# A fused two-block transformer kernel: order of values, scores and weight splits in the first block's head loop

## The chip, the cores and the metric

The kernel runs on one core of a Trainium2 chip. The time is that of the device for one execution, in microseconds (us). The engines are TensorE (PE, with its weight loads shown as PEld), VectorE (DVE), ScalarE (ACT), GpSimd (POOL) and SyncE (SP), which here only issues transfers.

## The reference

`x` has 512 tokens of 2048 features. The first block is sliding-window attention with 32 heads of 64 in 4 key/value groups, attention sinks, ALiBi and an output gate. The second block (two layers) is latent attention, a short convolution and memory attention, with a gate; it isn't touched here. Cut to the first block:

```
h = rmsnorm(x, g_pre)
q, k, v, z = split(h @ w_in)                     # 2048, 256, 256, 2048 columns
scores = q.k / 8 - slope * dist, masked to a window of 128, in blocks of 128 queries by 256 keys
p = softmax(concat(scores, sink))[..., :-1]
o = p @ v
y = (o * silu(z)) @ w_out
x = x + rmsnorm(y, g_post)
```

## The kernel before

Every weight matrix is handled in chunks of 2048 x 128 (1 MB), alternating between two slots of `raw`, `hi`, `lo` and `acc`. For each chunk SP loads `raw`; ACT writes `hi`, a rounded copy (`split` on ACT, L1147); DVE writes `lo = raw - hi` (`split` on DVE, L1599); PE then multiplies (`features`, L631): 16 k-tiles, each of three matmuls of 128 x 512 (hi by h_hi, hi by h_lo, lo by h_hi) into `acc[slot]`. A chunk can be split only when the chunk two before is multiplied (`chunk_done`), and multiplied only when `lo_done` says that it is split and `evacuated` that its accumulator has been read.

The first block's loop runs over 16 head pairs. Pair i has a q chunk (slot 0) and a gate chunk z (slot 1). Pair 0 stands before the loop, pairs 1 to 13 in it, and pairs 14 (`A`) and 15 (`B`) are written out behind it, where the order of chunks is q_a, q_b, z_a, z_b. In pair i:

- DVE scales q from the accumulator (`q_scaled`, L1786), ACT writes its high half (L1222), DVE its low half (`q_low`, L1792), which raises `q_split`.
- Inside the z chunk, ahead of k-tile 6, PE runs `scores_first(i)`: 16 matmuls of 256 columns (L781, L782). They wait for `q_split` and for POOL's copies of k (L533, L537).
- DVE runs `softmax_front(i)`: for each of the pair's two heads a large scalar_tensor_tensor over 128 x 1024 (L1747, scores from PSUM, `win` from SBUF), a maximum (L1749) and three tiny instructions (L1750 to L1752); ACT takes the exponentials (L1229, L1231); `softmax_back(i)` sums, inverts, scales (L1761 to L1764) and transposes 32 x 32 blocks into `pt1` (L1768).
- SP moves the transposed probabilities out to DRAM in two transfers (L390) and back in four (L393), `move_first(i)`. In SP's queue they stand between the load of a q chunk and the load of a gate chunk.
- Inside the z chunk of pair i+1, ahead of k-tile 10, PE runs `values_first(i)`: 16 matmuls (L795) with 64-column weights. They wait for the four transfers (`pt1_in`), for POOL's copy of v (`vcur`, L544) and for the earlier y product.
- DVE forms the y product (`y_first`, L1776, two instructions) and the gate (`gate_first`: L1802 reads the z accumulator and releases it, ACT takes tanh, L1237, DVE closes with L1806).

Each engine executes its own instructions in the order in which they are written. DVE's order for pair i before: split of z_i, q, split of q_(i+1), softmax_front(i), y_first(i-1), softmax_back(i), gate_first(i). Behind the loop it is: split of q_b, q(14), split of z_a, softmax_front(14), y_first(13), softmax_back(14) with the scaling of q_b inside, q_low(15), split of z_b, softmax_front(15), softmax_back(15). PE runs scores(14) and values(13) in q_b, scores(15) ahead of k-tile 10 of z_a, values(14) ahead of k-tile 3 of z_b.

Of the kernel before, what the change touches and what calls it, by code (L numbers as in the profile page):

```python
# [22 lines left out]
def build(nc, xT, memT, mem, pos, gains, gain_row, sinks, consts, window, w1, w2, out):  # L23
# [7 lines left out]
    ACT = mybir.ActivationFunctionType  # L31
# [4 lines left out]
    D, S, MEM = 2048, 512, 256  # L36
# [8 lines left out]
    PAIR1 = 4  # L45
# [40 lines left out]
    def chunk1(p, i=0):  # L86

        new = isinstance(i, int) and i == 0 and p < 2
        return Chunk(i * 2 + p, p % 2, i + p // 2, i + p // 2, None if new else 2)
# [57 lines left out]
    with ctx:  # L147
# [473 lines left out]
        def _(pe):  # L621
# [31 lines left out]
            def features(c, x_hi, x_lo, meanwhile=(), last_reader=False):  # L653

                begin(c)
                for k in range(KT):
                    for pause, other in meanwhile:
                        if k == pause:
                            other()
                    ins = k_tile(c, k, x_hi, x_lo, k == 0, k == KT - 1)  # L660
                    if last_reader and k == KT // 2 - 1:
                        ins.then_inc(h_half_read, 1)
                ins.then_inc(chunk_done, 1)
# [110 lines left out]
            def scores_first(i):  # L774
                pe.wait_ge(q_split, i + 1)
                pe.wait_ge(kcur_done, i * 3 + 3)
                for b in range(TB):
                    for par in range(2):
                        to = bank(2 * par + b // 2, 256, b % 2 * 256)
                        q, k = tile(par * TB + b, P), slice(b * P, b * P + 256)  # L780
                        pe.matmul(to, q1[:, q], k_hi[:, k], start=True, stop=False)  # L781
                        ins = pe.matmul(to, q1[:, q], k_lo[:, k], start=False, stop=True)  # L782
                ins.then_inc(scores1, 1)

            def values_first(i):
                pe.wait_ge(pt1_in, i * (QUADS * 16) + QUADS * 16)
                pe.wait_ge(vcur_done, i * 2 + 2)
                pe.wait_ge(y1, i + 1)
                for kb in range(TB):
                    at, n = 2 * kb * BLK, (2 if kb < TB - 1 else 1) * BLK  # L790
                    for par, rows_ in enumerate(HALVES):
                        to = ov[par][rows_, kb * P:kb * P + QUADS * n].rearrange("p (b a i) -> p a b i", a=QUADS, i=BLK)
                        src = pt1[:, 0:T1].rearrange("p (a n x) -> p a n x", a=QUADS, n=2)[:, :, par, at:at + n]
                        src = src.rearrange("p a (b i) -> p a b i", i=BLK)
                        ins = pe.matmul(to, vcur[:, kb * P + par * HD:kb * P + (par + 1) * HD], src,  # L795
                                        start=kb == 0, stop=kb == TB - 1, skip_group_check=True)
                ins.then_inc(values1, 1)

            def pair(i, first):

                features(chunk1(PAIR1, i), h_hi, h_lo,
                         meanwhile=[(9, lambda: spread(1, ov[1][:, 0:MEM], MEM, zt))] if first else [])
                features(chunk1(PAIR1 + 1, i), h_hi, h_lo,
                         meanwhile=[(6, lambda: scores_first(i))] if first else
                         [(6, lambda: scores_first(i)), (10, lambda: values_first(i - 1))])

            pair(0, True)
            with pe.Fori(1, A) as i:
                pair(i, False)
            features(q_a, h_hi, h_lo)  # L810
            features(q_b, h_hi, h_lo, meanwhile=[(6, lambda: scores_first(A)), (10, lambda: values_first(A - 1))])
            features(z_a, h_hi, h_lo, meanwhile=[(10, lambda: scores_first(B))])
            features(z_b, h_hi, h_lo, meanwhile=[(3, lambda: values_first(A))], last_reader=True)

# [327 lines left out]
        def _(act):  # L1142
            def split(c, width=CW):
                act.wait_ge(loaded[c.slot], (c.uses + 1) * 16)
                if c.back is not None:
                    act.wait_ge(chunk_done, c.n + (1 - c.back))
                act.activation(hi[c.slot][:, 0:width], raw[c.slot][:, 0:width], ACT.Copy).then_inc(hi_done, 1)  # L1147
# [70 lines left out]
            def q_hi(i, qc):  # L1218
                act.wait_ge(evacuated[qc.slot], qc.accs + 1)
                act.wait_ge(scores1, i + 1)  # L1220
                for par, half_ in enumerate(HALVES):
                    ins = act.activation(q1[half_, tile(par)], qt[half_, :], ACT.Copy)  # L1222
                ins.then_inc(q_hi_done, 1)

            def exps_first(i):
                for par in range(2):
                    act.wait_ge(shift1, i * 2 + (par + 1))
                    for n in range(par * TB, par * TB + TB):
                        act.activation(prob1[:, tile(n, 256)], prob1[:, tile(n, 256)], ACT.Exp,  # L1229
                                       bias=nm[:, n:n + 1], accum_out=ls[:, n:n + 1])  # L1230
                    act.activation(es[:, tile(par, TB)], es[:, tile(par, TB)], ACT.Exp).then_inc(exp1, 1)  # L1231

            def tanh_first(i, zc, first=False):
                act.wait_ge(evacuated[zc.slot], zc.accs + 1)
                if not first:
                    act.wait_ge(sg_done, i)
                act.activation(tz, zt[:, :], ACT.Tanh, scale=0.5).then_inc(tanh1, 1)  # L1237

            def pair(i, first):
                qc, zc = chunk1(PAIR1, i), chunk1(PAIR1 + 1, i)  # L1240
                split(zc)
                q_hi(i, qc)
                split(chunk1(PAIR1 + 2, i))
                exps_first(i)
                tanh_first(i, zc, first)

            pair(0, True)
            act.wait_ge(r_done, 2)
            act.activation(ones_r[:, :], ones, ACT.Copy)
            act.activation(r_mem[:, :], ov[1][:, 0:MEM], ACT.Copy).then_inc(r_mem_done, 1)  # L1250
            with act.Fori(1, A) as i:
                pair(i, False)
            split(q_b)
            q_hi(A, q_a)
            split(z_a)
            exps_first(A)
# [339 lines left out]
        def _(dve):  # L1596
            def split(c, width=CW):
                dve.wait_ge(hi_done, c.n + 1)
                dve.tensor_tensor(lo[c.slot][:, 0:width], raw[c.slot][:, 0:width], hi[c.slot][:, 0:width].bitcast(F32),  # L1599
                                  ALU.subtract).then_inc(lo_done, 1)  # L1600
# [140 lines left out]
            def softmax_front(i):  # L1741
                dve.wait_ge(scores1, i + 2)
                for par in range(2):
                    link = Links(soft1_link, i * 12 + par * 3)
                    half_, part = tile(par, 1024), tile(par, TB)
                    sink = snk[:, col(i * 2 + par)]
                    link.then(dve.scalar_tensor_tensor(prob1[:, half_], win[:, :], cst[:, col(i * 2 + (SLOPE + par))], sc[:, half_],  # L1747
                                                       ALU.mult, ALU.add))
                    link.then(dve.tensor_reduce(mx[:, part], prob1[:, half_].rearrange("p (n k) -> p n k", n=TB), AX.X, ALU.max))  # L1749
                    link.then(dve.tensor_scalar(mx[:, part], mx[:, part], sink, None, ALU.max))  # L1750
                    dve.tensor_scalar(es[:, part], mx[:, part], -1.0, sink, ALU.mult, ALU.add)
                    dve.tensor_scalar(nm[:, part], mx[:, part], -1.0, None, ALU.mult).then_inc(shift1, 1)  # L1752
# [47 lines left out]
            def gate_first(i, zc, meanwhile=None):  # L1800
                dve.wait_ge(chunk_done, zc.n + 1)
                dve.tensor_tensor(zt[:, :], acc[zc.slot][:, :], r_x[:, :], ALU.mult).then_inc(evacuated[zc.slot], 1)  # L1802
                if meanwhile is not None:
                    meanwhile()
                dve.wait_ge(tanh1, i + 1)
                dve.scalar_tensor_tensor(sg, tz, 1.0, zt[:, :], ALU.add, ALU.mult).then_inc(sg_done, 1)  # L1806

            def pair(i, first):
                zc = chunk1(PAIR1 + 1, i)
                split(zc)  # L1810
                q(i, chunk1(PAIR1, i))
                split(chunk1(PAIR1 + 2, i))
                softmax_front(i)
                if not first:
                    y_first(i - 1)
                softmax_back(i)
                gate_first(i, zc)

            def y_lo_tile(t, count):
                dve.wait_ge(y_hi_done, count)  # L1820
# [1 line left out]
                                  ALU.subtract).then_inc(y_done, 1)  # L1822

            dve.wait_ge(window_in, 32)
            pair(0, True)
            dve.wait_ge(x_stored, 16)
            with dve.Fori(1, A) as i:
                pair(i, False)
            split(q_b)
            q(A, q_a)  # L1830
            split(z_a)
            softmax_front(A)
# [688 lines left out]
```

## Time and profile before

| | us |
|---|---|
| median of 3 runs | 2197.26 (2196.68 to 2197.3) |
| the profiled execution | 2197.51 |
| its span | 2195.7 |
| PE busy | 2178.5 |
| PEld busy | 1818.9 |
| DVE busy | 1524.7 |
| ACT busy | 837.5 |
| POOL busy | 211.3 |

The span is the time from the first to the last instruction of the trace; the execution's own time is 1.8 us longer. Busy times are sums over the engine's instructions; matmul ends are modelled, so a short stop of PE can lie hidden between two matmuls whose records overlap, and the starts of the matmuls show it better. The granted clock of TensorE is at full speed, 0.999 on the mean. The head loop runs from about 60 to 480 us of the span.

### The profile page before, as it was taken

Reading aid. Unit: us, or ns where it says so; the run is one execution under the profiler, and the core shown is the slowest. Engines: PE = TensorE matmul, PEld = TensorE weight load, DVE = VectorE, ACT = ScalarE, POOL = GpSimd, SP = SyncE. Lnnn points to the kernel's source line nnn. Section 1 sums busy time; section 2 is a strip of 40 time slices with the busy share of each in tenths; the row PEclk is TensorE's granted clock in tenths of the full one; section 3 lists DMA queues with packets and bytes.
Section 4 is the critical chain, followed back from the end, with each engine's and each line's share of the span. In section 5 each row is a group of like instructions: output and inputs, shape, how many; then the busy total and the mean of one; then the engine's idle time right before and its main releaser. Section 6 shows DMA issues by size and latency. Waiting matters only on the chain.

```text
span 2195.7 us, 27821 instructions
## 1 busy us (share of the span) xinstructions
PE 2178.5 (99%) x10428; PEld 1818.9 (83%) x10428; DVE 1524.7 (69%) x2224; ACT 837.5 (38%) x1307; POOL 211.3 (10%) x215
## 2 busy tenths in 40 slices
PE   8999999999999999999999999999999999999998
PEld 7888888888888888888888888888888888888887
DVE  6677788888988543567677778786434677677665
ACT  6433433453345421334333533444213443435221
POOL 0100000114420100000000053201000000000000
PEclk9999999999999999999999999999999999999999
DMA  7445545442257223225443422573222154435532
GB/s 278 172 154 155 159 157 160 146 149 96 89 213 273 78 96 100 75 75 160 134 139 119 142 107 82 194 268 113 96 96 75 65 158 132 144 117 155 176 119 108
DMA packets 91019, 303.25 MB, mean 138 GB/s; under 512 B 7536, under 2 KB 48752, under 8 KB 67888
## 3 DMA queue, kind: packets, MB, share of 16 engines
q1 hardware_dynamic: 84912, 275.00, 38.0%
q10 hardware_dynamic: 4896, 17.30, 2.1%
q0 software_dynamic: 1120, 9.70, 1.2%
q8 instruction: 61, 1.00, 0.2%
q14 instruction: 30, 0.25, 0.0%
HBM read 253.74 MB, written 48.23 MB: 138 GB/s over the span
## 4 chain that ended last, share of the span: by engine, by line
PE 98%; DMA 1%; DVE 1%; issue 0%; ACT 0%; SPq 0%; DVEq 0%; POOLq 0%; POOL 0%; ACTq 0%
PE acc L631 69%; PE sc L631 11%; PE ov L631 6%; PE sc L855 3%; PE sc L856 2%; PE ov L795 1%; PE sc L782 1%; PE sc L781 1%; PE sc L1038 1%; PE sc L1037 1%; DMA g<-xT_dram 0%; PE acc L816 0%; PE acc L817 0%; PE acc L647 0%; PE acc L820 0%
## 5 line engine op out<-in xcount | busy, mean ns | idle before, releaser
L631 PE MATMUL acc<-h_all,hi 128*128 128x512 f32 x4160 | 1286.9, 391 | 8.9 <-DVE h_all L1691 8.9
L631 PEld LDWEIGHTS acc<-h_all,hi 128*128 128x128 f32 x4160 | 775.6, 188 | 170.5 <-issue 12.0
L631 PE MATMUL acc<-h_all,lo 128*128 128x512 f32 x2080 | 809.9, 389 | 0.0
L1599 DVE TENSOR_TENSOR lo<-raw,hi 128x2048 fp32r<-128x2048 f32 (+3 forms) x158 | 345.1, 2184 | 171.3 <-ACT hi L1147 169.2
L631 PEld LDWEIGHTS acc<-h_all,lo 128*128 128x128 f32 x2080 | 390.8, 188 | 81.9
L1147 ACT ACTIVATE hi<-raw 128x2048 fp32r<-128x2048 f32 (+3 forms) x158 | 289.1, 1830 | 430.5 <-PE acc L631 263.8
L1229 ACT ACTIVATE prob<-prob,st 128x256 f32<-128x256 f32 x128 | 63.6, 498 | 109.4 <-DVE st L1752 109.4
L631 PE MATMUL sc<-hi,h_all 128*128 128x512 f32 (+1 forms) x320 | 90.7, 369 | 0.0
L1306 ACT ACTIVATE hi<-raw 128x512 fp32r<-128x512 f32 x50 | 30.4, 627 | 120.7 <-PE sc L856 107.5
L631 PEld LDWEIGHTS sc<-hi,h_all 128*128 128x128 f32 x320 | 58.1, 189 | 10.4 <-issue 0.5
L1542 ACT ACTIVATE prob<-sc,st 128x512 f32<-128x512 f32 x64 | 44.2, 690 | 43.6 <-DVE st L2299 43.6
L496 POOL TENSOR_TENSOR sqacc<-sqacc,sq 128x512 f32<-128x512 f32 x28 | 53.4, 1907 | 57.9 <-ACT sq L1161 56.4
L631 PE MATMUL sc<-lo,h_all 128*128 128x512 f32 (+1 forms) x160 | 58.8, 368 | 0.0
L1154 ACT ACTIVATE hi<-raw 128x1024 fp32r<-128x1024 f32 x32 | 32.2, 1054 | 68.4 <-PE acc L631 54.3
L855 PE MATMUL sc<-t_parts,hi 128*128 128x512 f32 x160 | 57.8, 398 | 0.0
L2238 DVE TENSOR_TENSOR pt_low<-pt,pt_hi 128x1024 fp32r<-128x1024 f32 x32 | 37.8, 1222 | 25.8 <-ACT pt_hi L1504 25.8
L555 POOL TENSOR_TENSOR t_raw<-g 128x512 f32<-128x512 f32 x4 | 7.1, 1778 | 484.8 <-DVE lo L1599 484.8
L1504 ACT ACTIVATE pt_hi<-pt 128x1024 fp32r<-128x1024 f32 x32 | 32.1, 1052 | 48.4 <-DMA pt<-turned 48.4
L2298 DVE TENSOR_REDUCE st<-sc 128x1 f32<-128x512 f32 x64 | 44.1, 689 | 7.6 <-PE sc L1038 5.1
L1161 ACT ACTIVATE sq<-g 128x512 f32<-128x512 f32 x64 | 38.7, 627 | 22.5 <-POOL qacc L500 7.6
L608 POOL DMA_DIRECT2D cs<-gain_row_dram x1 | 0.6, 623 | 481.6 <-ACT h_all L1164 481.6
L2362 DVE STREAM_TRANSPOSE x_rows<-x_piece 32x512 f32<-32x512 f32 x64 | 45.0, 703 | 2.6 <-DMA x_piece<-residual 0.8
(331 smaller groups left out, 3399.3 us busy)
## 6 DMA issues: line engine op xcount, KB each, us to landing
raw<-w_dram SPq DMA_DIRECT2D x170, 1024.0 KB, 4.9
turned<-pt SPq DMA_DIRECT2D x32, 512.0 KB, 3.2
pt<-turned SPq DMA_DIRECT2D x64, 256.0 KB, 5.1
turned<-pt SPq DMA_DIRECT2D x32, 448.0 KB, 3.0
pt<-turned SPq DMA_DIRECT2D x64, 224.0 KB, 4.0
xr<-residual ACTq DMA_DIRECT2D x16, 512.0 KB, 5.2
residual<-g ACTq DMA_DIRECT2D x16, 512.0 KB, 4.7
raw<-w_dram SPq DMA_DIRECT2D x8, 896.0 KB, 6.6
```

Of the source, the lines that this page charges most:

```text
L496: pool.tensor_tensor(to[:, :], to[:, :], sq[:, tile(slot)], ALU.add).then_inc(added, 1)
L631: ins = pe.matmul(to, a, b, start=first and n == 0, stop=last and n == 2)
L855: pe.matmul(bank(bank_).rearrange("p (s n) -> p s n", s=2), high_, both, start=first and m == 0, stop=end, skip_group_check=True)
L856: ins = pe.matmul(bank(bank_, TILES), low_, both[:, 0, :], start=False, stop=end, skip_group_check=True)
L1147: act.activation(hi[c.slot][:, 0:width], raw[c.slot][:, 0:width], ACT.Copy).then_inc(hi_done, 1)
L1161: act.activation(sq[:, tile(slot)], src, ACT.Square).then_inc(squared, 1)
L1229: act.activation(prob1[:, tile(n, 256)], prob1[:, tile(n, 256)], ACT.Exp, bias=nm[:, n:n + 1], accum_out=ls[:, n:n + 1])
L1542: act.activation(prob2[:, tile(b)], bank(b), ACT.Exp, scale=MLA_SCALE, bias=nm[:, b:b + 1], accum_out=ls[:, b:b + 1]).then_inc(exp2, 1)
L1599: dve.tensor_tensor(lo[c.slot][:, 0:width], raw[c.slot][:, 0:width], hi[c.slot][:, 0:width].bitcast(F32), ALU.subtract).then_inc(lo_done, 1)
L2238: dve.tensor_tensor(keys_half(pt2_low, n), keys_half(pt2, n), keys_half(pt_hi, n).bitcast(F32), ALU.subtract)\
L2298: link.then(dve.tensor_reduce(mx[:, one], bank(b), AX.X, ALU.max))
L2362: dve.transpose(to[:, 4 * c:4 * c + 4, :, a, :], from_[:, :, :, q, :]).then_inc(x_turned, 1)
```

## The change

In the loop's z chunks and in q_b, the values of the pair before now stand ahead of k-tile 6 and the scores ahead of k-tile 7. On DVE softmax_back(i) follows softmax_front(i) directly; then comes the split of the next pair's gate weights (which moves from the next pair's start), then y_first(i-1), then gate_first(i). ACT's split of these weights moves likewise, from the next pair's start to directly behind the exponentials and ahead of tanh. The first gate chunk is split before pair 0, and the split of q_b that stood behind the loop is now the last one in it. Two small ACT copies (`ones_r`, `r_mem`) move from behind pair 0 into it. SP's and POOL's code is the same.

```diff
                 features(chunk1(PAIR1 + 1, i), h_hi, h_lo,
                          meanwhile=[(6, lambda: scores_first(i))] if first else
-                         [(6, lambda: scores_first(i)), (10, lambda: values_first(i - 1))])
+                         [(6, lambda: values_first(i - 1)), (7, lambda: scores_first(i))])
...
-            features(q_b, h_hi, h_lo, meanwhile=[(6, lambda: scores_first(A)), (10, lambda: values_first(A - 1))])
+            features(q_b, h_hi, h_lo, meanwhile=[(6, lambda: values_first(A - 1)), (7, lambda: scores_first(A))])
...
             def pair(i, first):                       # ACT
                 qc, zc = chunk1(PAIR1, i), chunk1(PAIR1 + 1, i)
-                split(zc)
                 q_hi(i, qc)
+                if first:
+                    act.wait_ge(r_done, 2)
+                    act.activation(ones_r[:, :], ones, ACT.Copy)
+                    act.activation(r_mem[:, :], ov[1][:, 0:MEM], ACT.Copy).then_inc(r_mem_done, 1)
                 split(chunk1(PAIR1 + 2, i))
                 exps_first(i)
+                split(chunk1(PAIR1 + 3, i))
                 tanh_first(i, zc, first)
 
+            split(chunk1(PAIR1 + 1))
             pair(0, True)
-            act.wait_ge(r_done, 2)
-            act.activation(ones_r[:, :], ones, ACT.Copy)
-            act.activation(r_mem[:, :], ov[1][:, 0:MEM], ACT.Copy).then_inc(r_mem_done, 1)
             with act.Fori(1, A) as i:
                 pair(i, False)
-            split(q_b)
...
             def pair(i, first):                       # DVE
-                zc = chunk1(PAIR1 + 1, i)
-                split(zc)
                 q(i, chunk1(PAIR1, i))
                 split(chunk1(PAIR1 + 2, i))
                 softmax_front(i)
+                softmax_back(i)
+                split(chunk1(PAIR1 + 3, i))
                 if not first:
                     y_first(i - 1)
-                softmax_back(i)
-                gate_first(i, zc)
+                gate_first(i, chunk1(PAIR1 + 1, i))
...
+            split(chunk1(PAIR1 + 1))
             pair(0, True)
             dve.wait_ge(x_stored, 16)
             with dve.Fori(1, A) as i:
                 pair(i, False)
-            split(q_b)
```

## Rows read from the trace of the kernel before

**Rows 1.** The page, busy time of each engine.
```profile
PE 2178.5 (99%) x10428; PEld 1818.9 (83%) x10428; DVE 1524.7 (69%) x2224; ACT 837.5 (38%) x1307; POOL 211.3 (10%) x215
```

**Rows 2.** Waits of PE's weight loads, 80 to 500 us: total us, times, longest.
```profile
PEld ov L795 <- issue: 5.6, 16, 0.4
PEld acc L631 <- issue: 2.7, 16, 0.2
PEld acc L631 <- DVE lo L1599: 0.2, 1, 0.2
```

**Rows 3.** Timeline of PE, one loop period: start us, duration us, instruction, count.
```profile
220.20 0.62 PE L631 MATMUL acc<-h_all,hi 128*128 128x512 f32 x2
...
224.28 0.28 PE L781 MATMUL sc<-k_hi,q 128*128 128x256 f32 x1
...
226.08 0.28 PE L782 MATMUL sc<-k_lo,q 128*128 128x256 f32 x1
...
228.72 0.39 PE L631 MATMUL acc<-h_all,lo 128*128 128x512 f32 x1
229.03 1.73 PE L795 MATMUL ov<-pt,vcur 128*64 128x256 f32 x16
...
231.50 0.62 PE L631 MATMUL acc<-h_all,hi 128*128 128x512 f32 x2
...
249.87 0.28 PE L781 MATMUL sc<-k_hi,q 128*128 128x256 f32 x1
```

**Rows 4.** Timeline of DVE over the same period, idle before in brackets.
```profile
226.66 1.27 DVE L1747 SCALAR_TENSOR_TENSOR prob<-win,cst,sc 128x1024 f32<-128x1024 f32 x1
...
232.77 0.47 DVE L1751 TENSOR_SCALAR st<-st,snk 128x4 f32<-128x4 f32 x1
...
233.22 1.38 DVE L1776 SCALAR_TENSOR_TENSOR g<-ov,sq 64x512 f32 x2
...
238.80 1.11 DVE L1768 STREAM_TRANSPOSE pt<-prob 128x896 f32<-128x896 f32 x1
239.94 0.69 DVE L1802 TENSOR_TENSOR zt<-acc,sqacc 128x512 f32<-128x512 f32 x1
241.33 0.69 DVE L1806 SCALAR_TENSOR_TENSOR sq<-sq,zt 128x512 f32<-128x512 f32 x1 [0.70 <-ACT sq L1237]
243.14 2.29 DVE L1599 TENSOR_TENSOR lo<-raw,hi 128x2048 fp32r<-128x2048 f32 x1 [1.11 <-ACT hi L1147]
...
248.10 1.39 DVE L1792 TENSOR_TENSOR q<-dg,q 64x512 fp32r<-64x512 f32 x2 [1.42 <-ACT q L1222]
```

**Rows 5.** ACT and POOL over this period; line L1751: ns min/median/max.
```profile
235.32 0.19 ACT L1231 ACTIVATE st<-st 128x4 f32<-128x4 f32 x1
...
232.58 0.63 POOL L537 CAST k_lo<-k_lo_all 64x512 fp32r x1 [0.26 <-POOL k_hi L533]
...
L1751 DVE TENSOR_SCALAR st<-st,snk x26: 228/347/624, 101.6 to 411.9; 128x4 f32<-128x4 f32 x26
```

**Rows 6.** SP's queue in this period; time from issue to landing of L393.
```profile
242.90 1.76 SPq L393 DMA_DIRECT2D pt<-turned  x4
245.61 0.36 SPq L357 DMA_DIRECT2D raw<-w_dram  x1
...
DMA to landing us min/median/max: 3.1/4.1/5.0
```

**Rows 7.** Behind the loop: DVE, PE's weight load, the fourth transfer, its landing.
```profile
431.30 1.27 DVE L1747 SCALAR_TENSOR_TENSOR prob<-win,cst,sc 128x1024 f32<-128x1024 f32 x1
...
444.84 1.39 DVE L1792 TENSOR_TENSOR q<-dg,q 64x512 fp32r<-64x512 f32 x2
...
448.54 1.28 DVE L1747 SCALAR_TENSOR_TENSOR prob<-win,cst,sc 128x1024 f32<-128x1024 f32 x1
...
446.28 0.19 PEld L781 LDWEIGHTS sc<-k_hi,q 128*128 128x128 f32 x1
...
424.33 0.43 SPq L393 DMA_DIRECT2D pt<-turned  x1
...
pt<-turned SPq DMA_DIRECT2D x1, 224.0 KB, 4.3
```

## The prediction, made before the changed kernel was run

> **What bounds the kernel now.** I read the page's busy line first: TensorE (PE) is busy for all but 17 us of the span [rows 1]. Then the waits of the PE weight loads between 80 and 500 us, the stretch that the change touches: one wait for a DVE weight split, 0.2 us, and short stops around each values group [rows 2]. So the loop is at PE's own rate and has nearly nothing to give back; what matters is whether the new order makes PE wait. For that I read one period on PE [rows 3], then DVE, ACT, POOL and SP over the same period [rows 4 to 6], then the loop's exit [rows 7]. The period is 249.87 - 224.28 = 25.59 us. The gate chunk starts at 220.20 (call this z0) and scores are six tiles later, 4.08 us, so a k-tile is 0.68 us. A values group starts 0.08 us late (228.72 to 229.03 is 0.31 where 0.23 is the pitch), and it and the tile behind it take 231.50 - 229.03 = 2.47 us. DVE has slack, but in two places little: its split of the next gate weights ends at 243.14 + 2.29 = 245.43, and PE loads weights for that chunk at about 220.20 + 25.59 - 0.23 = 245.56; the low half of q ends at 248.10 + 1.39 = 249.49, and PE loads for the scores at 249.87 - 0.23 = 249.64.
>
> **PE's own work.** The loop issues the same matmuls. Values stood between two accumulation tiles and still do: at tiles 6 and 7 one k-tile lies between values and scores. So the same switches are paid: 0 us. As bounds, dropping the 0.08 us and the weight load's stop behind each group (2.7 us / 16 = 0.17) [rows 2] would give 14 x 0.25 = 3.5 us; paying them once more would cost as much. The rows have the same neighbours, so I take 0.
>
> **Where scores and softmax land in the loop.** New scores start at z0 + 4.08 + 0.08 + 2.47 = z0 + 6.63, instead of z0 + 4.08. The group's first to last start is 226.08 - 224.28 = 1.80 and the last matmul lasts 0.28, so they end at z0 + 8.71 and DVE's first softmax instruction starts near z0 + 8.75 = 228.95. Before, it started at 226.66 [rows 4]: 2.29 us later. From there to the y product took 233.22 - 226.66 = 6.56. In it one tiny tensor_scalar (L1751) took 0.47, beside a POOL copy, where the shortest of its line takes 0.23 [rows 4, 5]. In the new order POOL copies vcur directly after values and k after scores, beside the first large softmax instruction, so I take 6.32 (bounds 6.32 and 6.56). The Trainium skill's GPSIMD Engine Reference, Specifications, says that POOL's SBUF interface is shared with VectorE and contends when DVE has two SBUF inputs or a two-port mode. The large instruction reads win from SBUF and scores from PSUM, so by that rule it is spared too; if it were slowed like L1751, the margin below would be gone. The y products (two, 1.39 together) now stand behind; softmax back takes 239.94 - 233.22 - 1.41 = 5.31. ACT's exponentials ended at 235.32 + 0.19 [rows 5] and now end 2.05 to 2.29 us later, by 237.8; DVE needs the second half's at half of 5.31 behind 235.27, 237.9. They hide, if by little; 0.3 us would be lost at worst. The second transpose, before 238.80 + 1.11 = 239.91, now ends at 228.95 + 6.32 + 5.31 - 0.03 = 240.55: 0.64 us later.
>
> **The added risk: probabilities for values.** Values were due at z0 + 8.83; they are now due at z0 + 25.59 + 4.16 = 249.95, 4.67 us earlier in the chunk. SP's queue is q weights, two transfers out, four in, gate weights. The second out goes at the transpose's end (239.91), the first in follows at 242.90, 2.99 later [rows 6]; the fourth is issued some 1.3 later (1.76 for all four) and lands up to 5.0 after its issue: about 249.2. Plus 0.64 that is 249.85, against 249.95. The margin is 0.1 us (0.25 with the loop's usual 4.9 and the first decimal of the view). I take a loop stall of 0. The gate weight load now waits for nothing (its split is done before) and goes directly behind the four transfers, 0.9 us nearer to them than 245.61 is to 242.90 + 1.76. I know no row with this order that landed later, and cost it at 0, at worst 0.3 us per period. The skill's DMA: Bandwidth & Descriptors, Anatomy of one DMA, fits a transfer as 2.0 us plus bytes over 436 GB/s. By it a 448 KB out is 3.05 us, as the trace has (2.99), but four loads of 224 KB would have landed 4.1 us after the first issue, where the trace has 6.3; by the page values would have 2 us to spare, and the loop rival below would have no chance. The measurement decides.
>
> **Splits, y, gate.** ACT's split of the next gate weights follows the exponentials: 237.6 + 1.9 = 239.5, before DVE is free at 240.55. DVE: split to 242.9, y to 244.3, gate product to 245.0. PE needs that accumulator and those weights at 245.56, so 0.55 us are left for the accumulator (its product ended at 240.6 before) and 2.7 us for the weights (0.13 before). Tanh and the second gate product end near 244.3 + 241.33 - 239.94 + 0.69 = 246.4, where q's chunk is done near 246.0; so q's scaling starts up to 0.4 later and q's low half ends at 249.9; the scores need it only at 245.79 + 6.4 = 252.2. All hidden. The 0.2 us wait of [rows 2] goes; it is one of a weight load, which hides most of it behind the matmuls in flight, so I take 0 (at most -0.2). The two small ACT copies of pair 0 move ahead of q_1's weight split; no values group follows in that pair, so its softmax may be late by their time: 0.
>
> **The exit of the loop.** This is where I find a cost. The values of the loop's last head pair, values(13) during q_b, are due at 424.92 (scores at 249.87 + 7 x 25.59 = 429.00, less 4.08) + 4.16 = 429.08. Their fourth transfer was issued at 424.33 and landed 4.3 later, 428.63 [rows 7]; this iteration issues it late. Plus 0.64 and 0.05 for the signal: 429.32, a stall of 0.24. Scores(14) then end at 429.32 + 2.47 + 2.08 = 433.87 and DVE's softmax starts at 433.91 instead of 431.30: 2.61 later. From 431.30 to the low half of q_b at 444.84 + 1.39 = 446.23 DVE runs without a gap (softmax front, y, softmax back with q_b's scaling in it, low half), and this order is not changed. PE's scores(15) at z_a's tile 10 wait for it already: their weight load is at 446.28, 0.05 behind DVE, and only 0.06 later than it would be without a wait. With DVE 2.61 later, PE waits to 448.89: PE loses 2.6 us, the 0.24 included. Then all else moves with it: DVE's z_b split and next softmax (448.54 before) by the same 2.6, and the values of head pair 14, whose transfers follow softmax back directly, keep the place that they have to them now. PE is the bound to the end of the span [rows 1], so nothing gives it back.
>
> **Sum.** +2.6 (exit, one time) + 0 (PE's work) + 0 (loop, splits) = +2.6 us. The profiled execution took 2197.51 us for a span of 2195.7, so 2200.1 for one like it; it lies 0.25 above the median, 2197.26. Predicted: 2199.9 us. A difference under 0.2%, 4.4 us, is about what a measurement of this kernel can't tell from none.
>
> **Rivals.**
> A. The loop is caught by the probabilities. From scores' end the ring is DVE, transfers out and in, values, one tile, scores; I make it 25.59 - 0.1. Each 0.1 us over that costs 12 x 0.1, from head pair 1 on. With L1751's 0.24 back: +0.14 a period, 1.7 us, 2201.6. With 0.3 us of transfer contention alone: +0.2, 2.4 us, 2202.3. With both: 0.44 x 12 = 5.3, 2205.2. It is slower by over 0.2% from 0.15 us a period on (1.8 us). For it: the margin is smaller than the spread of landings (4.7 to 5.0 over the iterations). Against: these landings are steady, and the first three transfers already keep all DMA engines busy, so that a load behind them has little to push aside. Chance 0.27, of which 0.19 over the 0.2%.
> B. No loss at the exit: scores(15) doesn't wait, or DVE makes up the 2.6 us. The time is 2197.2. For it: PE's gap there is only 0.06 us in the trace and a releaser is not named. Against: DVE has no idle time on that stretch to make up with. Chance 0.08.
> C. Values and scores near each other save the switches: 14 x 0.25 = 3.5 us against the 2.6: 2196.4; with B as well 2193.8, below the 0.2%. For it: PE pays 0.25 us a group. Against: a k-tile lies between. Chance 0.07.
> The forecast itself has 0.58.
>
> The range goes from 2196.8 (B, half of C) to 2203.0 (A with either cause alone, by nothing more); 2 in 10 or less stay outside. Slower by over 0.2% 0.19, faster 0.03, within 0.78.
>
> **What would show it.** In the changed profile: PE's wait for DVE's q low half before the last scores group, 2.4 us, and a small one for transfers before values(13); loop period 25.59 still; gate split ending 2.7 us ahead of PE; the gate product ending half a us ahead of it. The prediction is wrong if the period is longer (A), if PE waits at the gate chunk's start for the accumulator, or if scores(15) start without a wait.

## The result and the profile after

The changed kernel takes 2204.62 us (median of 7, 2202.59 to 2206.24) against 2197.3 before: a ratio of 1.0032, 95% interval 1.0022 to 1.0041. That is slower, clear of the noise, and above the stated range (2196.8 to 2203.0). Its executions also scatter more: 3.6 us from first to last, before 1.5. The profiled execution took 2202.66 us, near the lowest, for a span of 2200.8. So what follows in this section accounts for 5.15 of the 7.3 us; part of the rest shows in the trace of the run with the gate weight load held back.

PE's work is the same as in [rows 1], the rest of the longer span is time in which it stands still:

```profile
PE 2179.9 (99%) x10428; PEld 1821.5 (83%) x10428; DVE 1518.6 (69%) x2224; ACT 837.2 (38%) x1307; POOL 215.3 (10%) x215
```

The waits of PE and of its weight loads between 80 and 500 us (total us, times, longest), to set beside [rows 2]. Before, there was no wait of PE's matmuls in this stretch:

```profile
PE sc L781 <- DVE q L1793: 2.1, 1, 2.1
PE ov L795 <- DMA pt<-turned: 0.6, 2, 0.4
PE ov L795 <- issue: 0.5, 3, 0.2
...
PEld ov L795 <- issue: 7.2, 14, 0.8
...
PEld sc L781 <- DVE q L1793: 2.5, 1, 2.5
PEld ov L795 <- DMA pt<-turned: 0.7, 2, 0.4
```

Two costs can be read: one stop of 2.1 us before a scores group, and many small ones before values groups. The small ones are mostly not shown as waits, since the record of the matmul before still overlaps; the starts show them. PE's timeline, one loop period, as in [rows 3], with the first and last scores group of the loop:

```profile
100.00 0.28 PE L781 MATMUL sc<-k_hi,q 128*128 128x256 f32 x1
...
251.62 0.39 PE L631 MATMUL acc<-h_all,lo 128*128 128x512 f32 x1
252.14 1.73 PE L795 MATMUL ov<-pt,vcur 128*64 128x256 f32 x16
...
254.60 0.28 PE L781 MATMUL sc<-k_hi,q 128*128 128x256 f32 x1
...
277.75 1.73 PE L795 MATMUL ov<-pt,vcur 128*64 128x256 f32 x16
...
280.22 0.28 PE L781 MATMUL sc<-k_hi,q 128*128 128x256 f32 x1
...
434.73 0.28 PE L781 MATMUL sc<-k_hi,q 128*128 128x256 f32 x1
```

Before the values group at 252.14 the gap is 0.52 us where it was 0.31. Scores to scores over the loop is (434.73 - 100.00) / 13 = 25.75 us, before 25.59. The stops beyond the usual 0.09 sum to 2.6 us over the 14 values groups from 97.54 on, of which 0.5 stands before the first.

DVE in this period, as in [rows 4]:

```profile
256.83 1.28 DVE L1748 SCALAR_TENSOR_TENSOR prob<-win,cst,sc 128x1024 f32<-128x1024 f32 x1 [2.35 <-PE sc L782]
...
262.94 0.23 DVE L1752 TENSOR_SCALAR st<-st,snk 128x4 f32<-128x4 f32 x1
...
267.31 1.11 DVE L1769 STREAM_TRANSPOSE pt<-prob 128x896 f32<-128x896 f32 x1
268.35 2.25 DVE L1600 TENSOR_TENSOR lo<-raw,hi 128x2048 fp32r<-128x2048 f32 x1
270.52 1.38 DVE L1777 SCALAR_TENSOR_TENSOR g<-ov,sq 64x512 f32 x2
271.93 0.69 DVE L1803 TENSOR_TENSOR zt<-acc,sqacc 128x512 f32<-128x512 f32 x1
```

and SP's queue, as in [rows 6]:

```profile
271.42 1.76 SPq L393 DMA_DIRECT2D pt<-turned  x4
273.38 0.36 SPq L357 DMA_DIRECT2D raw<-w_dram  x1
```

DVE waits for scores, runs the softmax in one piece, and the second transpose ends 11.59 us after its start (forecast 11.60). The small instruction took 0.23 here instead of 0.47. The transfers in are issued 3.00 us behind it, and the gate weight load 0.2 us behind the last of them.

This is a ring: scores 254.60, softmax 256.83 (2.23), transposes 268.42 (11.59), transfers in 271.42 (3.00), values 277.75 (6.33), scores 280.22 (2.47), together 25.62 us. PE's own period is 25.59. The ring is the longer one, by 0.03 here and by 0.16 on the mean. The 6.33 us from the first transfer in to the values are 6.10 until the last of the four has landed, at 277.52, and 0.23 until PE's first matmul.

The stop behind the loop, with DVE's start of softmax(14), its low half of q_b, and PE's weight load for scores(15), as in [rows 7]:

```profile
436.84 1.28 DVE L1748 SCALAR_TENSOR_TENSOR prob<-win,cst,sc 128x1024 f32<-128x1024 f32 x1 [2.12 <-PE sc L782]
...
450.39 0.69 DVE L1793 TENSOR_TENSOR q<-dg,q 64x512 fp32r<-64x512 f32 x1
...
451.83 0.19 PEld L781 LDWEIGHTS sc<-k_hi,q 128*128 128x128 f32 x1 [2.51 <-DVE q L1793]
```

DVE starts when scores(14) end and then runs nearly without a gap; PE waits for what it does last.

### The profile page after: what moved, and what is told of

The parts are those of the page before. It is cut to its first block, busy times and chain, and to the rows that moved or that the text cites. A ratio compares the mean times of both kernels' runs of the same rounds, so it can differ in the third digit from the quotient of the medians.

```text
span 2200.8 us, 27834 instructions
## 1 busy us (share of the span) xinstructions
PE 2179.9 (99%) x10428; PEld 1821.5 (83%) x10428; DVE 1518.6 (69%) x2224; ACT 837.2 (38%) x1307; POOL 215.3 (10%) x215
## 4 chain that ended last, share of the span: by engine, by line
PE 95%; DVE 3%; DMA 1%; issue 1%; SPq 0%; ACT 0%; POOL 0%; DVEq 0%; POOLq 0%
PE acc L631 65%; PE sc L631 12%; PE ov L631 6%; PE sc L855 3%; PE sc L856 2%; PE ov L795 1%; PE sc L781 1%; PE sc L782 1%; PE sc L1038 1%; PE sc L1037 1%; DMA pt<-turned 0%; DMA g<-xT_dram 0%; PE acc L816 0%; PE acc L817 0%; PE acc L650 0%
## 5 line engine op out<-in xcount | busy, mean ns | idle before, releaser
L1748 DVE SCALAR_TENSOR_TENSOR prob<-win,cst,sc 128x1024 f32<-128x1024 f32 x32 | 40.9, 1277 | 32.9 <-PE sc L782 32.9
L544 POOL COPY vcur<-vall 128x256 f32 x32 | 17.2, 562 | 312.8 <-PE ov L795 312.5
```

## The experiments

All are timed beside the kernel before on the same chip; its median was 2197.4, 2197.46 and 2197.35 us in the three groups.

**The changed kernel again**, beside the next three.

> The changed kernel once more, on the chip of the three others, to have its time beside theirs and a second trace. Ring theory (loop bound by the ring scores, softmax, transfers, values, one tile, scores): 2202.6 to 2206, more spread than before, with the period near 25.75 us and up to 25.95 in slower executions, and one stop of 2.1 to 2.5 us before scores(15). If the 2 us between the profiled execution and the median are noise of the first runs, it comes at 2202.7.

2205.61 us (5 runs, 2202.83 to 2207.48), ratio 1.0035 (1.0022 to 1.0049). Its profiled execution took 2203.56: the period is (435.48 - 100.79) / 13 = 25.75 again, the stop before scores(15) 2.1 us again. The result repeats; most executions again lie above the profiled one. Of the changed kernel's 12 executions in both groups four have a mean granted clock of 0.998 or less, and they took 2205.61 to 2207.48 us; the other eight took 2202.59 to 2205.61, their median is 2204.0. What the lower mean stands for is seen in the trace of the run with the gate weight load held back.

**Exit: q_b's old placement.**

```diff
-            features(q_b, ..., meanwhile=[(6, lambda: values_first(A - 1)), (7, lambda: scores_first(A))])
+            features(q_b, ..., meanwhile=[(6, lambda: scores_first(A)), (10, lambda: values_first(A - 1))])
```

> Only q_b's placement goes back: scores(14) ahead of tile 6, values(13) ahead of tile 10. Exit theory (scores(15) wait for DVE, which started softmax(14) 2.2 to 2.6 us late): 2.1 to 2.4 us less than the changed kernel, no stop before scores(15), loop as in the changed kernel (2202.3 by its median). If DVE is late there for another reason (the loop's own lateness of q), less than 1 us is gained.

2201.69 us (11 runs, 2200.21 to 2203.52), ratio 1.0019 (1.001 to 1.0028), 3.9 below the changed kernel beside it, 2.9 below its first median. PE's waits, 80 to 500 us:

```profile
PE ov L795 <- DMA pt<-turned: 1.9, 4, 0.9
PE sc L781 <- DVE q L1793: 0.2, 1, 0.2
```

The stop before scores(15) goes from 2.1 to 0.2 us (by the starts from 2.24 to 0.41); the loop's stay, with a mean period of 25.76. The exit is a cause of its own. The medians gave more than the 2.1 to 2.4 expected. All 11 executions have a mean granted clock of 0.999; against the eight of the changed kernel with 0.999 or more the gain is 2.3 us, the size that was expected.

**Values and scores next to each other.**

```diff
-                         [(6, lambda: values_first(i - 1)), (7, lambda: scores_first(i))])
+                         [(6, lambda: values_first(i - 1)), (6, lambda: scores_first(i))])
(and in q_b likewise)
```

> Values and scores both ahead of tile 6, values first, in the loop and in q_b: the one k-tile between them goes, everything else as in the changed kernel. Ring theory: the ring is 0.68 us shorter, so 25.1 to 25.3 against PE's 25.59: the loop's stalls vanish (-2.1 against the trace, up to -4.8 against the median), and the exit's is 0.7 less; 2198.8 to 2199.5. Contention theory (the gate weight load behind the four transfers delays them by a varying amount): the stall is mostly gone too, but landing times are above 5.0 in some periods. Switch theory (PE loses by the new neighbours, not by waits): no gain over the changed kernel, 2203 to 2205.

2200.3 us (11 runs, 2198.87 to 2202.55), ratio 1.001 (1.0001 to 1.0019). Twelve periods in a row are 25.55 or 25.56 us:

```profile
252.40 0.39 PE L631 MATMUL acc<-h_all,lo 128*128 128x512 f32 x1
252.72 1.73 PE L795 MATMUL ov<-pt,vcur 128*64 128x256 f32 x16
254.38 0.39 PE L781 MATMUL sc<-k_hi,q 128*128 128x256 f32 x1
...
278.27 1.74 PE L795 MATMUL ov<-pt,vcur 128*64 128x256 f32 x16
```

Scores now start 1.66 us behind values, before 2.47. This takes 0.8 us out of the ring and ends every stall inside the loop: values come 0.32 us after the tile before, as in the kernel before. What stays is at the ends: 0.7 us before values(0), 0.6 before values(13), 1.4 before scores(15) (1.6 by the starts). The median came 0.8 us above the upper end of what I expected; I had priced none of the first two. The profiled execution is the slowest of its 11, 2202.55 us: its granted clock was half from 14.3 to 17.7 us of the span, long before the loop, and its scores(0) start at 74.92, 2.3 us later than in the kernel before. By their starts the new neighbours also save PE 0.03 us a period.

**DVE's and ACT's order alone.**

```diff
-                         [(6, lambda: values_first(i - 1)), (7, lambda: scores_first(i))])
+                         [(10, lambda: values_first(i - 1)), (6, lambda: scores_first(i))])
(and in q_b likewise)
```

> DVE's and ACT's new order alone; on PE scores ahead of tile 6 and values ahead of tile 10 as before. Ring theory: values are due 2.7 + 3.4 us later in the ring than they were in the changed kernel, so no stall, and the exit has none: 2197.3, within 0.3 us of before. If DVE's new order costs by itself (gate product late for PE, q late for the scores: both still have over half a microsecond in the changed trace, but scores are due 2.55 us earlier here, at z0 + 4.08, where q's low half ends at about z0 + 4.1): 0.1 to 0.3 us a period, up to 2201.

2197.4 us (11 runs, 2197.01 to 2198.37), ratio 1.0 (0.9991 to 1.0009), no wait of PE's matmuls in the stretch, periods of 25.59. This half of the change costs nothing and gives nothing: PE is the bound without it. The loss comes with PE's placement; how large it gets depends on DVE's order, as the next two runs show.

**PE's placement alone**, on the kernel before.

```diff
-                         [(6, lambda: scores_first(i)), (10, lambda: values_first(i - 1))])
+                         [(6, lambda: values_first(i - 1)), (7, lambda: scores_first(i))])
(and in q_b likewise)
```

> PE's new placement (values at 6, scores at 7) with DVE's and ACT's order of before. Ring theory: y_first (1.41) and the slowed small instruction (0.24) stand in the ring again, and, longer still, the gate weight split comes last on DVE: from softmax start 13.28 to the gate product, 3.2 to the split, 2.3 for it, and then PE's 6 tiles, values, tile, scores: about 27.8 us a period by my sum, 2.2 over PE's 25.59. 13 periods make 28 us: 2224 to 2228 with the exit. Contention or switch theory: DVE's order matters only in slack, so within 2 us of the changed kernel, 2203 to 2207.

2226.87 us (4 runs, 2226.18 to 2226.95), ratio 1.0135 (1.0119 to 1.0151). The waits name the ring that I had taken for the longer one, through the split of the gate weights, and the period is (430.64 - 99.29) / 12 = 27.61 us, against my 27.8:

```profile
PE acc L631 <- DVE lo L1599: 22.6, 13, 1.7
PE sc L781 <- DVE q L1792: 2.1, 1, 2.1
```

With PE's new placement DVE's and ACT's new order is worth 21 to 22 us (2226.87 against 2204.62 and 2205.61); with the old placement it is worth nothing.

**y between the two halves of softmax**, in the changed kernel.

```diff
                 softmax_front(i)
+                if not first:
+                    y_first(i - 1)
                 softmax_back(i)
                 split(chunk1(PAIR1 + 3, i))
-                if not first:
-                    y_first(i - 1)
```

> The changed kernel with y_first back between softmax front and back; the gate weight split stays ahead. Ring theory: the transposes come 1.41 to 1.65 us later and the ring, which binds already, grows by all of it: 12 or 13 x 1.4 to 1.65 = 17 to 21 us over the changed kernel, 2222 to 2226; PE waits for the transfers, not for DVE's split. If the loop isn't a ring and only the due time of the values counts, one such delay is paid once a period too, but not more than 0.2 to 0.4 us behind the slack: 2205 to 2209.

2222.7 us (4 runs, 2222.02 to 2224.79), ratio 1.0115 (1.0099 to 1.0131), 17 to 18 over the changed kernel:

```profile
PE ov L795 <- DMA pt<-turned: 22.9, 15, 2.7
PE sc L781 <- DVE q L1793: 2.1, 1, 2.1
```

Work of 1.4 us put into the ring comes out in every period, whose mean over 12 goes from 25.76 to 27.25: the ring binds already. With the split ahead, PE waits for the transfers and no longer for the split, so the two rings of the last experiment are told apart.

**Both three tiles earlier**, one tile between them as in the changed kernel.

```diff
-                         [(6, lambda: values_first(i - 1)), (7, lambda: scores_first(i))])
+                         [(3, lambda: values_first(i - 1)), (4, lambda: scores_first(i))])
(and in q_b likewise)
```

> The changed kernel with values ahead of tile 3 and scores ahead of tile 4, in the loop and in q_b. Both move three tiles (2.04 us) forward in the chunk together. Ring theory: the ring's length is the same, so the loop's stalls are as before this edit; at the exit DVE starts softmax(14) only 0.5 us later than in the kernel before instead of 2.6, so the stop before scores(15) shrinks by 2.0: 2202.5 to 2203.7. Due-time theory (values are due 2.04 us earlier in the chunk, transfers come when they come): 12 x 2 us more, 2225 or over.

2202.26 us (10 runs, 2201.8 to 2204.39), ratio 1.0023 (1.0014 to 1.0033). Values are due 2 us earlier in every chunk, and the loop's period is (408.00 - 98.58) / 12 = 25.79 us, against 25.75 before the edit. The place in the chunk costs nothing, the distance from values to scores does. Once, the earlier place is paid: 1.6 us before values(0), since pair 0 has its scores ahead of tile 6 still. The stop before scores(15) is nearly gone, 0.2 us by the starts.

```profile
PE ov L795 <- DMA pt<-turned: 3.5, 5, 1.6
PE ov L795 <- issue: 0.3, 2, 0.2
...
PEld sc L781 <- DVE q L1793: 0.5, 1, 0.5
```

**The gate weight load behind the landed transfers.**

```diff
                 move_first(i - 4)
+                sp.wait_ge(pt1_in, i * (QUADS * 16) - 3 * (QUADS * 16))
                 load1(1, i)
```

> The changed kernel, but SP issues the gate weight load only when the four transfers of probabilities have landed (one more wait in SP's queue), so nothing runs behind them. Contention theory: landings become shorter and steadier; 1.5 to 4 us less than the changed kernel (2201 to 2203) and less spread. Ring theory with uncontended transfers (the landings in the changed trace, 4.8 to 5.0, are those of before): no change, 2204 to 2206, and the same spread. The load itself has some 13 us to spare until its split.

2202.14 us (11 runs, 2200.31 to 2203.31), ratio 1.0019 (1.001 to 1.0028): 2.5 below the changed kernel's first median, 3.5 below its second. SP in one period:

```profile
269.87 1.76 SPq L393 DMA_DIRECT2D pt<-turned  x4
276.19 3.07 SPq L357 DMA_DIRECT2D raw<-w_dram  x2
```

Time from issue to landing of the transfers in, min/median/max, from 100 to 445 us, first of the changed kernel, then of this one:

```profile
DMA to landing us min/median/max: 3.0/4.0/5.0
```
```profile
DMA to landing us min/median/max: 2.9/4.0/4.8
```

By each period's own times (12 periods of the loop) the last of the four lands 6.03 us behind the first issue, where it was 6.23, and the loop's mean period falls to (432.28 - 99.50) / 13 = 25.60. The ring was so near PE's period that this decides it. I had expected no change by the ring theory with undisturbed transfers; that part of it falls, for the landings that I took as undisturbed were not. In the kernel before, with the gate weight load 1.0 us behind the transfers instead of 0.2, the last landed 6.21 us behind the first issue, and the view from 100 to 445 us is the same 3.0/4.0/5.0. What costs 0.2 us is that the load follows at all; that the change brought it nearer cost 0.02.

This profiled execution took 2202.8 us, no less than the changed kernel's, though its loop is 2 us shorter. The difference is a stretch at half clock right behind the exit's stop. PE's timeline, and its granted clock in three stretches (start and end, length, PE busy, PEclk, DMA share, GB/s):

```profile
449.39 0.38 PE L782 MATMUL sc<-k_hi,q 128*128 128x256 f32 x1 [2.10 <-DVE q L1794]
449.61 0.28 PE L783 MATMUL sc<-k_lo,q 128*128 128x256 f32 x1
449.73 0.28 PE L782 MATMUL sc<-k_hi,q 128*128 128x256 f32 x1
...
450.92 0.41 PE L783 MATMUL sc<-k_lo,q 128*128 128x256 f32 x1
451.13 0.41 PE L782 MATMUL sc<-k_hi,q 128*128 128x256 f32 x1
```
```profile
440.00:450.00 10.00, 7.90 (x38) 1.00 0.23 79
450.10:453.50 3.40, 3.40 (x16) 0.50 0.48 121
453.60:460.00 6.40, 6.40 (x33) 1.00 0.86 260
```

PE had stood still for 2.1 us before 449.39. From 450.1 to 453.5 the granted clock is 0.50, the lower level (1.2 GHz instead of 2.4), and a scores matmul follows the one before after 0.21 us instead of 0.12. Scores(15) to values(14) is 9.77 us, in the changed kernel's trace 8.25: the stretch costs 1.5 us. The trace of the run with y between the halves has such a stretch too, from 452.1 to 455.5; there PE stood still for 2.7 us until 452.56. The two traces of the changed kernel have the same exit stop and none, so the stop doesn't always bring one. Of the 31 executions of the four versions whose traces show a stop of 2.1 us or more between 440 and 480 us, the changed kernel among them, 8 have a mean granted clock of 0.998 or less; of the 138 of the kernel before in the three groups and of the other versions without such a stop, 2 (the version with values and scores next to each other, 2 of 11, is in neither count). That the stop brings the lower clock fits this; no run here separates the two.

**Exit and gate load together.**

> The changed kernel with both single edits that helped: q_b's old placement (exit) and the gate weight load behind the landed transfers. If exit and loop contention are separate causes, their gains add: 2205 - 3.5 - 3 = 2198 to 2199; what is left over the kernel before is the stop before values(0), 0.4 to 0.9 us, and periods up to 0.05 us over 25.59. If they are one cause (a later DVE reads as both), the sum gains no more than the larger of them: 2201 to 2202.

Both edits, as above: 2198.21 us (11 runs, 2197.97 to 2201.09), ratio 1.0006 (0.9997 to 1.0015). It is 6.4 and 7.4 below the changed kernel's two medians, where the single edits gave 2.9 to 3.9 and 2.5 to 3.5: the gains add, as far as the scatter lets it be told. In the stretch one wait of PE's matmuls is left:

```profile
PE sc L782 <- DVE q L1794: 0.2, 1, 0.2
```

**Values directly behind scores**, with DVE's new order, and on the kernel before.

```diff
+                         [(6, lambda: scores_first(i)), (6, lambda: values_first(i - 1))])
(and in q_b likewise)
```

> The changed kernel's DVE and ACT order, with scores and then values both ahead of tile 6: values directly behind scores. They are due at z0 + 6.0, where the transfers land near z0 + 2: no ring. A period was 25.555 us where values and scores stood next to each other the other way round, 0.03 under 25.585. Switch theory (neighbours save one switch, in either order): 14 x 0.03 = 0.4 us less than before, 2196.9 to 2197.0. If only that order saved it: 2197.4.

2197.93 us (11 runs, 2197.4 to 2199.42), ratio 1.0003 (0.9994 to 1.0012).

> The kernel before, all engines in their old order, with values moved from tile 10 to tile 6, directly behind scores. The transfers land near z0 + 3.4, values are due at z0 + 6.0, so no wait is added in the loop. Switch theory: 0.4 us less than before, 2196.9 to 2197.0, if PE's trace shows 25.555 a period. If the y product, whose values now end 2.7 us earlier, or anything else of DVE binds, 2197.4 or more.

2197.68 us (11 runs, 2196.49 to 2199.63), ratio 1.0002 (0.9993 to 1.0011). In both the period is 25.60 us, 0.01 longer than before and not 0.03 shorter: only scores behind values saved PE something. Neither is faster than the kernel before, and no version was.

## Why the prediction was wrong

**The exit** was right in mechanism and nearly in size. Forecast 2.6 us, of which 2.4 before scores(15) and 0.24 before values(13); the trace has 2.24 by PE's starts (2.08 as a wait) and nothing extra before values(13), whose transfers were not issued late in that execution. The edit that undoes it gave 2.9 to 3.9 us of the medians, but 2.3 among executions of the same mean granted clock. What was not in the forecast is that the stop can be followed by a stretch at half clock, 1.5 us more where a trace shows it.

**PE's own work** at 0 was right: the same neighbours, the same gaps. The bound of 3.5 us for the switches was far too wide; next to each other they save 0.4 us in the loop or nothing, by the order.

**DVE's order, splits and gate** were right: transposes 11.59 us behind the start of softmax, gate product ended at 272.62, some 0.7 us ahead of PE's next gate chunk (values at 277.75, less six tiles, the stop and the weight load: 273.3), and DVE's order by itself at 2197.4.

**The step that failed is the loop stall at 0.** I compared a landing at 249.85 with values due at 249.95 and called a margin of 0.1 us enough. Added up as the ring that it is, the forecast was 25.48 us against PE's 25.59. In us, the last two columns being means of 12 periods, from the starts and landings of the traces:

| | forecast | changed kernel | gate load held back |
|---|---|---|---|
| scores start to softmax start | 2.12 | 2.23 | 2.23 |
| softmax start to second transpose's end | 11.60 | 11.59 | 11.60 |
| to the first transfer in | 2.99 | 3.00 | 3.00 |
| to the landing of the last | 6.30 | 6.23 | 6.03 |
| landing to first values matmul | 0 | 0.25 | 0.28 |
| values start to scores start | 2.47 | 2.47 | 2.47 |
| sum, unrounded | 25.48 | 25.76 | 25.60 |

The term that the forecast put at nothing is the restart: PE's first values matmul starts 0.23 or 0.28 us behind the landing, in every one of these 12 periods. I had counted 0.05 for a signal at the exit and nothing in the loop. The second is the softmax, which starts 0.11 us later behind the scores than I took: 0.44 us behind the start of their last matmul in the loop, and only behind the loop 0.32. Both together, less 0.07 us by which the landings came sooner than the latest one that I had taken, turn +0.11 into the measured -0.17. The gate weight load is not among the missing terms: that it comes nearer was priced at 0 and cost 0.02, since the 0.2 us that it costs at either distance stood in the landings that I had read. But my reason, that a load behind busy engines has nothing to push aside, was wrong, and holding the load back is what brings the ring down to PE's period again.

So rival A is what happened, beside the exit: the ring of probabilities binds. It had 0.27, and its size was worked out by causes that weren't the ones: the small instruction's 0.24 did vanish, and the landings were no later than those of before. Its two single sizes, 1.7 and 2.4 us, are near the 2.1 us that the longer period costs, by luck. Its own top, 2205.2, lay outside the range that I gave; in a ring so near to PE's period its whole width belonged inside. The stop before values(0), 0.5 us in the trace and 0.2 to 1.0 in the others with the same placement, I had not priced at all: the first transfers in of the loop took 3.50 us to issue there, before 1.77. Why SP is slower in that first iteration is open.

**The sum.** Trace against trace, scores(15) come 451.83 - 446.42 = 5.4 us later: 2.2 exit, 2.6 values groups, and scores(0) that are 0.7 later already (73.27 against 72.61), ahead of anything that the change touches; without any change there they lie between 72.2 and 73.6 in all traces but the one with the early stretch at half clock. Some 0.3 us come back until the end of the span. For the medians, 7.3 us: undoing exit and load removes 6.4 of it; 0.9 is left, with an interval that includes none. That the median lies 2 us above the profiled execution is in part the stretch at half clock, which 4 of the 12 executions have by their mean granted clock. The other eight still have a median of 2204.0, 0.5 and 1.4 above the two profiled ones; what makes up this rest is not known.

## What to carry to other kernels

A kernel whose one engine is busy 99% of the time gains nothing from moving work off the others' critical paths, but it can lose: before such a move, follow the work around the whole ring and compare its length with the engine's period. Put every handover into that sum, the restart behind a landing too (0.25 us here): a margin smaller than these is no margin. The distance between the two groups inside the loop sets the ring's length; their place in the chunk only moves what is paid at entry and exit. And a stop of 2 us on an engine that is otherwise always busy can cost more than itself, when the granted clock falls behind it: read the clock of the slower executions before looking for another wait.

## What was not expected of the hardware

- A 1 MB load issued behind four loads of 224 KB from the same queue delays the last of them by 0.2 us (6.23 us behind the first issue, 6.03 with the load held back), although it is queued behind them. Whether it is issued 0.2 or 1.0 us behind them makes no difference to be seen (6.23, 6.21).
- Between the landing of a transfer and the first matmul that waited for it lie 0.23 to 0.28 us; between the start of the last scores matmul and DVE's first instruction on its result lie 0.44 in the loop and 0.32 behind it, where the forecast took 0.32.
- In two traces the granted clock falls to half for a stretch, in one right behind a stop of PE of 2.1 us and in one near the end of a stop of 2.7 us, in the middle of dense work. In the first it cost 1.5 us. In other traces the same stop passes without it.
- A scores group directly behind a values group (128 x 64 weights) makes a period 0.03 us shorter than with one tile between; the other way round it is 0.01 longer.
- The last of four 224 KB loads lands 6.2 us behind the first issue (1.3 + 4.9), where the fit that the prediction quotes from the Trainium skill's DMA: Bandwidth & Descriptors gives 4.1. The section gives that fit for one transfer issued from GpSimd; for these four, issued by SP, the trace shows that it doesn't hold.
